# Decode keys transposed in 32x32 blocks by VectorE, and w_out multiplied partly during decode, with the rest computed by tokens

## What is computed

```
# decode, for each of the 8 sequences: 4 queries on 1024 paged past keys + the new ones
s = q @ k.T * 128**-0.5 + (c_q - c_k)        # c: cumulated log-forget; causal among the new tokens
o_fox = softmax(s) @ v                        # keys, values: 8 pages of 128 tokens x (6 heads x 128)
o_mem = softmax(q_m @ mk.T * 128**-0.5) @ mv  # 256 memory keys, 4 heads
# all 288 tokens
cat = concat[o_fox (6 heads), o_hgrn (6 heads) , o_mem (4 heads)]   # 16 heads x 128 = 2048
h = x + cat @ w_out                           # w_out 2048 x 2048, 16.8 MB
logits = rmsnorm(h) @ w_router                # 4 groups + 32 experts, then top-2 experts
y = h + sum over 2 experts (silu(hn @ w_gate) * (hn @ w_up)) @ w_down    # 32 experts, 403 MB
```

## Time and profile before

| | |
|---|---|
| median of 3 runs | 1857.64 us |
| profiled execution | 1856.99 us, its span 1855.3 us |
| TensorE busy | 1487.9 us (80%), 9493 matmul records |
| weight loads busy | 886.0 us (48%) |
| VectorE, ScalarE, GpSimd busy | 433.8, 222.3, 77.9 us |
| moved by DMA | 555.09 MB, mean 299 GB/s |
| decode | about 574 to 746 us |
| w_out and router logits | 745.6 to 898.3 us |
| routing and gather | 898 to 917 us |
| experts | 917 to the end |

### The profile page before, as it was taken

One profiled execution on the slowest core, in us unless ns is written; L12 is line 12 of the kernel. 1 busy time (PEld: TensorE's weight loads), 2 busy tenths in 40 slices (PEclk: granted clock), 3 DMA queues, 4 the chain that ended last, 5 costly groups with the idle time before them and its releaser, 6 DMA issues.

```text
span 1855.3 us, 23473 instructions
## 1 busy us (share of the span) xinstructions
PE 1487.9 (80%) x9493; PEld 886.0 (48%) x9493; DVE 433.8 (23%) x1137; ACT 222.3 (12%) x511; POOL 77.9 (4%) x141
## 2 busy tenths in 40 slices
PE   7999999999998999999867576576765667666746
PEld 6877777777776676777523141221312213122211
DVE  3016674532243333011301102012010020110201
ACT  3010101013323332111300000000000000000000
POOL 1000000310002221000000000000000000000000
PEclk9999999999999998999888788788887887787878
DMA  7642342432426997726399999999999999999996
GB/s 238 204 132 78 115 138 82 141 118 91 170 96 228 348 396 277 236 93 272 149 429 427 428 427 428 429 428 428 428 428 429 430 427 429 428 429 429 427 426 228
DMA packets 130332, 555.09 MB, mean 299 GB/s; under 512 B 13844, under 2 KB 83541, under 8 KB 104853
## 3 DMA queue, kind: packets, MB, share of 16 engines
q1 hardware_dynamic: 121988, 517.82, 70.1%
q0 software_dynamic: 8272, 36.25, 5.4%
HBM read 545.32 MB, written 8.72 MB: 299 GB/s over the span
## 4 chain that ended last, share of the span: by engine, by line
PE 65%; DMA 29%; DVE 2%; issue 1%; SPq 1%; ACT 1%; DVEq 0%; POOL 0%; ACTq 0%
PE PS L1720 20%; PE PS L2255 16%; DMA arena<-in_w_up_e_dram 9%; DMA arena<-in_w_down_e_dram 8%; DMA arena<-in_w_gate_e_dram 8%; PE PS L2296 7%; PE PS L2188 7%; DMA arena<-in_cache_mem_k_dram 3%; PE PS L2060 2%; PE PS L1775 1%; PE PS L2120 1%; DMA arena<-in_x_prompt_dram 1%; PE PS L2219 1%; PE PS L2077 1%; PE PS L2235 1%
## 5 line engine op out<-in xcount | busy, mean ns | idle before, releaser
L2255 PE MATMUL PS<-arena 128*32 128x512 f32 x1792 | 289.1, 727 | 200.1 <-DMA arena<-in_w_up_e_dram 128.9
L1720 PE MATMUL PS<-arena 128*128 128x288 f32 (+1 forms) x1728 | 445.5, 406 | 1.0 <-ACT arena L907 0.5
L1720 PEld LDWEIGHTS PS<-arena 128*128 128x128 f32 x1728 | 320.7, 191 | 93.4 <-issue 20.7
L2255 PEld LDWEIGHTS PS<-arena 128*32 128x32 f32 x1792 | 69.7, 131 | 411.2 <-issue 194.7
L2296 PE MATMUL PS<-arena 128*32 128x512 f32 x872 | 141.2, 731 | 112.5 <-DMA arena<-in_w_down_e_dram 112.5
L2255 PE MATMUL PS<-front,arena 128*32 128x512 f32 x256 | 145.4, 733 | 0.0
L2296 PEld LDWEIGHTS PS<-arena 128*32 128x32 f32 x872 | 37.5, 131 | 210.0 <-issue 123.4
L2188 PE MATMUL PS<-arena 128*128 128x288 f32 x512 | 130.8, 415 | 0.4 <-DVE arena L1481 0.4
L2188 PEld LDWEIGHTS PS<-arena 128*128 128x128 f32 x512 | 97.8, 193 | 32.3 <-issue 5.5
L1644 DVE TENSOR_TENSOR arena<-arena,PS 128x512 f32<-128x512 f32 (+1 forms) x96 | 65.6, 683 | 157.8 <-PE PS L2235 157.8
L1634 DVE TENSOR_TENSOR arena<-arena,PS 128x512 f32<-128x512 f32 x8 | 5.5, 688 | 405.9 <-PE PS L2255 405.9
(11 more groups left out here) (351 smaller groups left out, 1196.8 us busy)
## 6 DMA issues: line engine op xcount, KB each, us to landing
arena<-in_w_gate_e_dram SPq DMA_DIRECT2D x56, 2048.0 KB, 14.9
arena<-in_w_up_e_dram SPq DMA_DIRECT2D x56, 2048.0 KB, 15.1
arena<-in_w_down_e_dram SPq DMA_DIRECT2D x53, 2048.0 KB, 15.4
arena<-in_cache_fox_k_dram SPq DMA_DIRECT2D x64, 384.0 KB, 8.5
arena<-in_cache_fox_v_dram POOLq DMA_DIRECT2D x64, 384.0 KB, 7.1
arena<-in_w_in_dram SPq DMA_DIRECT2D x6, 3072.0 KB, 10.9
arena<-in_w_out_dram SPq DMA_DIRECT2D x8, 2048.0 KB, 9.1
front<-in_w_gate_e_dram SPq DMA_DIRECT2D x8, 2048.0 KB, 23.5
```

What stands on the lines that cost most here:

```text
L1720: last = pe.matmul(PS[0:m, bank, 0:w], wt[:, k, c:c + m], rhs[:, k, :], start=(k == 0), stop=(k == KC - 1))
L2255: last = pe.matmul(PS[x * SLOTS:(x + 1) * SLOTS, which, :], xgT[:, kk, x * SLOTS:(x + 1) * SLOTS], wt[:, k, :], start=(kk == 0), stop=(kk ...
```

## The change

It has five parts.

- **Keys.** A key page is transposed by one VectorE instruction in 32x32 blocks, from SBUF to SBUF. The blocks leave token groups of 32 and head slices of 32 on the partitions, so the queries are laid out block-diagonally (`q_diag`) and the scores run over 8 products on each of three strips, two heads in a strip. TensorE still transposes the memory keys (2 units). The decay rows are rearranged once by 16 small DMAs from SBUF to SBUF (`decay_b`).
- **Values.** The new order of the scores asks for values by token groups of 32: a page now goes to 32 partitions with 4 tokens each (`vhalf`), in rows of 3 KB as before. Three half-batch buffers take the place of two whole ones.
- **HGRN rows of w_out in decode.** One token tile of 128 by one column block of 512 per batch (`hgrn_prompt`), and the sample's columns on strips (`hgrn_sample`), put between the softmax steps where the key units were; VectorE adds each to x in `h_tok` (`filler_added`). x, the router's weights and these rows of `w_out` are loaded during decode.
- **Other rows of w_out, by tokens.** `cat` is the stationary operand and 512 columns of `w_out` move, so the result has tokens on the partitions; nothing is transposed back. Two of the eight prompt tiles run in the last batch, the other six and four sample blocks after it.
- **Router.** The gain is multiplied into the router's weights once; logits are made tile by tile, tokens on the partitions, from transposed blocks.

Core of the diff (the layout of buffers, constants and the order of expert loads are cut):

```diff
+        vhalf = [view(WORK + s * 4 * FW, 4, FW) for s in range(VHALF)]
+        keysB = view(WORK + 12 * FW, 4 * HF, NPG, 32)
+        wo_hgrn = [view(o, HG, 512) for o in (RAW + 5184, RAW + 8256)]
+        wo_rest = [view(o, HF + HM, 512) for o in (RAW + 1088, WORK + 9472, WORK, WORK + 9472)]
...
 # sync: the key pages of batch b + 1 wait for kt_dve instead of kt_filled
+            sp.wait_ge(decay_set, 1 + NPG)
+            for t in range(2):
+                old = decay[HB * t:HB * (t + 1), 0:PAST].rearrange("p (g a k) -> p a g k", a=4, k=32)
+                for a in range(4):
+                    sp.dma_start(decay_b[HB * a:HB * (a + 1), t, 0:PAST // 4]..., old[:, a]).then_inc(x_again, 16)
+                    sp.dma_start(decay_b[HB * a:HB * (a + 1), t, PAST // 4:], decay[...]).then_inc(x_again, 16)
...
+            for g in range(2):
+                load_key_page(1, g)
+            sp.wait_ge(gate_done, 2)
+            load_wo_hgrn(0)
             for t, (t0, n) in enumerate(TILES):
                 sp.dma_start(h_tok[0:n, t, :], x_tok_d[t]).then_inc(x_again, 16)
+            for g in range(2, NPG):
+                load_key_page(1, g)
+            load_mem_keys(1)
+            load_wo_hgrn(1)
+            for b in range(2, NB):
+                for g in range(NPG):
+                    load_key_page(b, g)
+                load_mem_keys(b)
+                if b in (4, 6):
+                    sp.wait_ge(fill_done, b - 2)
+                    load_wo_hgrn(b // 2)
...
 # gpsimd
+            def load_values(b, g):
+                half = 2 * b + g // 4
+                if half >= VHALF and g % 4 == 0:
+                    pool.wait_ge(d_pv, (half - VHALF) // 2 + 1)
+                page = pool.value_load(...)
+                pool.dma_start(vhalf[half % VHALF][32 * (g % 4):32 * (g % 4) + 32],
+                               v_pages[ds(page, 1)].rearrange("g (a k) n -> k (g a) n", a=4)).then_inc(v_in[b % 2], 16)
...
 # vector
+            def page_out(b, g):
+                dve.wait_ge(k_in[g], b * 16 + (32 if g < 6 else 16))
+                dve.transpose(keysB[:, :, g, :], kpage[g].rearrange("p (n d) -> p n d", d=32)).then_inc(kt_dve, 1)
...
             for b in range(NB):
                 decode_max(b)
                 if b + 1 < NB:
                     queries(b + 1)
+                pages_out(b + 1, (0,))
+                strips_max(b)
+                pages_out(b + 1, (1,))
+                max_set(b)
+                if b:
+                    heads_out(b - 1)
+                pages_out(b + 1, (2, 3))
+                probs_out(b)
+                decode_sums(b)
+                pages_out(b + 1, (4, 5, 6))
+                filler_added(b)
+                pages_out(b + 1, (7,))
...
 # tensor
+            def hgrn_prompt(b, k):
+                n, t = divmod(b, 2)
+                if k == 0:
+                    pe.wait_ge(wo_in[n % 2], 16 * (n // 2 + 1))
+                    if b:
+                        pe.wait_ge(fill_added, b)
+                last = pe.matmul(PS[:, 2, :], cat[:, 6 + k, t * P:(t + 1) * P], wo_hgrn[n % 2][:, k, :], ...)
...
+                if more:
+                    mem_keys_in(b + 1, 0)
+                hgrn_prompt(b, 0)
+                max_row(b)
+                hgrn_prompt(b, 1)
+                rest_rows(0, 1)
+                max_spread(b)
+                hgrn_prompt(b, 2)
+                hgrn_sample(b, 3 * (b % 2))
+                hgrn_prompt(b, 3)
+                rest_rows(2, 3)
+                probs_in(b)
+                hgrn_prompt(b, 4)
+                hgrn_sample(b, 3 * (b % 2) + 1)
+                if more:
+                    mem_keys_in(b + 1, 1)
+                hgrn_sample(b, 3 * (b % 2) + 2)
+                hgrn_prompt(b, 5)
+                rest_rows(*range(4, HF + HM))          # only in the last batch
                 decode_values(b)
                 if more:
                     decode_scores(b + 1)
+                else:
+                    rest_prompt(0, 1, range(HF + HM))
                 decode_heads(b)
...
+            rest_sample(0)
+            advance(0)                                  # transposes of a tile, logits of the one before
+            for n in range(1, 4):
+                rest_sample(n)
+                advance((1, 5, 8)[n - 1])
+                for t in range(2):
+                    rest_prompt(n, t, range(5))
+                    advance(((2, 4), (6, 7), (9, 10))[n - 1][t])
+                    rest_prompt(n, t, range(5, HF + HM))
...
-                    for k in range(KC):
-                        c = (n % 2) * P
-                        last = pe.matmul(PS[:, n % 2, 0:T], wo_slot[(n // 2) % 3][:, k, c:c + P], cat[:, k, :], ...)
-                if 1 <= n <= KC:
-                    by_token(n - 1)
```

## The result

The changed kernel takes 1934.48 us (median of 4, 1932.82 to 1938.59) against 1857.8 us (4 runs, 1854.47 to 1860.16): ratio 1.0426, 95% interval 1.0409 to 1.0442. The forecast was 1840.7 and its range ended at 1881, so the kernel is 93.8 us above the forecast and outside the range. The profiled span is 1933.3 us.

The account below looks back on a forecast made before the run. DMA was taken to bound decode and the expert stream, TensorE alone w_out. Decode's delay of +38.5 us and 55.4 us saved up to the logits gave -16.9 on 1856.99, shown as 1840.7 us; range 1808 to 1881.

Parts of the forecast that it names:

- value pages 23.6 MB ... I take 290, near the middle: 81.4 us: Decode DMA: value pages to 32 partitions move at 290 GB/s, between bounds of 175 and 397, taking 81.4 us.
- the two x_sample landings: Only earlier 32-partition load: 0.262 MB landing 1.5 us after x_prompt both times, read as 175 GB/s.
- neighbours in the queue would cover part: Decode DMA: key pages to all partitions alternate with value pages and cover part of their slowness; hence 290 GB/s.
- rival B: Decode's DMA queue: value pages stay as slow as x_sample even in company; 1883.5 to 1894 us, chance 0.24.
- the two new waits of a batch: Decode: TensorE's w_out products wait for the sum before, VectorE's sum for these products; costed at nothing, otherwise 7 us.
- rival A: Decode: value pages run at full rate, 59.4 us; last scores at 740.4, kernel 1819 us, chance 0.27.
- Last scores to logits: Stretch after decode, all on TensorE: 174.4 us before, 119.0 forecast, saving 55.4 us.
- Loads are no bound here: From last scores to logits: loads do not limit, since 18 MB move in 80 us.
- the block transpose: VectorE in decode: one 768-column block transpose per page taken at 1.03 us, eight making 8.3 us a batch.
- the products in decode hidden: Decode: TensorE's batch with the added w_out products, 18.7 us, stays under the 24 us of DMA.
- the tail: After the logits: the experts' stream only shifts, so this stretch stays unchanged at 957 us.
- sixteen decay DMAs: Before decode on SP: about 0.4 us each to issue, about 7 us ahead of the last w_in load, costed at nothing.

Follow-up runs that it names:

- e2: Changed kernel with the next batch's memory key units moved behind the softmax steps and last w_out product: 1885.18 us, ratio 1.0166.
- e12: Changed kernel with value pages on partitions 4k+q, probabilities permuted by two exponentials, memory keys behind the softmax: 1824.73 us, ratio 0.9825.
- e3: Changed kernel with value pages to all 128 partitions (values misplaced) and memory keys behind the softmax: 1821.43 us, ratio 0.9821.
- e6: Kernel before the change, with only 48 of 64 value pages loaded to 32 neighbouring partitions (values misplaced): 1910.25 us, ratio 1.031.
- e9: e8 with decode's prompt HGRN products moving 32 of 512 columns; total 5302 us not comparable, seventh values start at 744.74 against 745.44 us.
- e4: Changed kernel with value pages on partitions 4k+q and score products reading keys in matching, strided order: 1846.36 us, ratio 0.9956.
- e10: e2 with a batch's eight value pages issued in the order 0, 2, 1, 3, 4, 6, 5, 7: 1875.57 us, ratio 1.0101.
- e5: e4 plus the edit of e2 (memory keys behind the softmax): 1837.52 us, ratio 0.99.
- e8: Changed kernel with value pages on partitions 4k+q, VectorE's block transposes writing in 16-byte steps, memory keys behind the softmax: 1834.72 us, ratio 0.9891.

## Why the prediction was wrong

1. **The failed step: "value pages 23.6 MB ... I take 290, near the middle: 81.4 us".** With the holes away, the place costs e2 - e12 = 60.5 us (e2 - e3 = 63.8). Over the 59.4 us at full rate that is 119.9 us for 23.6 MB, 197 GB/s (123.2 us, 192 GB/s, by e3); e6 gives 183 in a kernel without any other part of the change. My lower bound was 175, from the two x_sample landings, and it was nearly the answer. One of the two was misread: the x_prompt half before the first x_sample was issued at 10.6 and took 15.8 us, so it landed at 26.4 and not at 26.2, and x_sample came about 1.3 us later, some 200 GB/s. So the two landings, 175 and about 200, stand on either side of what was measured. They should have outweighed the argument that neighbours in the queue would cover part; nothing in the trace had shown such cover. Mis-sized by 60.5 - 22.0 (what 81.4 already held over 59.4) = 38.5 us. The changed kernel's rate is rival B's (0.24). B gave 1883.5 to 1894, and e2, which has the slow pages without the wait of point 2, measured 1885.2; B's price for the whole change was too low by that wait.

2. **The missing step: the wait at the head of TensorE's batch, 49.3 us (change against e2).** I priced "the two new waits of a batch", those of the new products and of their sums, and overlooked a third, so that it stood at nothing: the next batch's memory keys, the last load of a batch in SP's queue, now stand ahead of the softmax, on which VectorE's transposes and through them the key loads depend. It was visible in the list of TensorE's steps. Before, units of the next batch stood between the steps as well, but those were key pages; the two memory key units were the last of the 14, behind `probs_in`. And at full rate they found their data there: from 590 to 724 us TensorE waited 3.5 us for memory keys and 4.6 for key pages in all.

3. **Sum.** The forecast without what it held for slow pages is 1840.7 - 22.0 = 1818.7. Measured is e12's 1824.7, plus 60.5 for the place and 49.3 for the wait, 1934.5. So the error of 93.8 is 38.5 + 49.3 + 6.0. The 6.0 stand behind the last scores. These begin at 741.9 in e12 (rival A said 740.4), but from there to the logits it takes 126.7 us, forecast 119.0, and 5.85 of them are TensorE's wait for `w_out` rows (point 4); e3, which takes 117.9 without such a wait, stands 2.7 above. The second exponential, which only e12 has, shows no cost before the last scores: e3 begins them at 741.9 too.

4. **Last scores to logits**: 130.9 us, forecast 119.0. In e2 it is 927.43 - 809.48 = 118.0, so the sum of steps came out (as a sum; its terms are not shown one by one); in the changed kernel 10.27 us is TensorE's wait for `w_out` rows. They are issued at 844.9, when VectorE's last block transpose (843.89 + 0.96) frees their place, and the wait ends at 865.4. In e12 they are issued at 740.0, again right behind the last transpose, and the wait is 5.9 us. "Loads are no bound here" was wrong by this much: it counted the volume and not when the place comes free.

5. **Right**: the block transpose 0.95 us (I took 1.03), with VectorE busy only 49.7 of 150 us; the products in decode hidden (e9, in e8's order); the tail 955.8 (957.0); the start: sixteen decay DMAs take 0.8 us each on SP (I took 0.4), the last w_in load is issued at 528.05, and the first scores begin at 583.4, before at 586.6. The trade itself pays once the two causes are away: decode grows by 18.0 us in e12 and in e3, and the stretch behind it shrinks by 47.7 and 56.5 (forecast 55.4).

The Trainium skill, page "SBUF — State Buffer", section "Door 1: The DMA port swizzle", has 218 GB/s at best for such pages, from which the prediction worked out 1867 us as an estimate. The runs' cost stands below that rate (183 to 197), nearer to the 189 GB/s that the page's table has as measured for 1 MiB on partitions 0 to 31. By its formula partitions 4k + q reach all 16 ports, and e4 agrees (5.9 us in place of 14.1). That two transfers to different halves do not add up stands in the same page's section "Can I just issue two DMAs to hit both halves?", which measured 6% for such a pair; e10, where pages to different halves are neighbours in the queue, gains 10 us of the 60 and agrees but for that small part.

## What to carry to other kernels

When an operand's new order changes which partitions a load writes, price the load by the nearest row of the same shape, in company too, and if it must go to few partitions, spread these over the whole range; pay for the permutation on the smallest array (here the probabilities, 0.5 us a batch against 3.6 on the keys' products and 4.9 on their transposes; e12 is 13 us under e5 and 10 under e8). On an in-order engine list what is queued behind each wait for a load, and follow it until it comes back to a load: a wait for late data ahead of what frees the buffers turns a slow transfer into an idle one.

## What the runs showed of the hardware

- Pages of 128 rows of 3 KB, four to a partition, on 32 neighbouring partitions: a cost as of 183 to 197 GB/s in company and a median landing of 12 to 14 us; on every fourth partition: 5.9 to 8.1 us and full rate (e12 382 GB/s in decode), with the same rows.
- A slow queue also slows the packets of the other queue: q1 moved 286 and 312 GB/s of its engine time beside slow value pages (the change, e2), 380 beside fast ones (e12).
- A moving fp32 operand read with 128 bytes between neighbours: 24 score products of 256 columns in 7.27 us in place of 3.63.
- A block transpose of 128x768 fp32 by VectorE: 0.95 us, and 1.56 us with a write step of 16 bytes.
